# Two attention heads in two halves of the array: unpadded queries, values by query block, o rounded one slot later

## The reference, cut to what matters

```python
def index_scores(qi, wi, ki, qpos, kpos):
    s = einsum('bthd,bsd->bths', qi, ki) * (IDX_DIM ** -0.5)
    s = einsum('bths,bth->bts', relu(s), wi)
    return where(kpos <= qpos, s, MASK_VALUE)
def forget_attend(q, k, v, Fq, Fk, qpos, kpos):
    logits = einsum('bthd,bshd->bhts', q, k) * (HEAD_DIM ** -0.5)
    logits = logits + (Fq[..., None] - Fk[..., None, :])
    logits = where(kpos <= qpos, logits, MASK_VALUE)
    return einsum('bhts,bshd->bthd', softmax(logits), v)
```

## Time and profile before

| | us |
|---|---|
| three runs: median (lowest, highest) | 1118.53 (1115.49, 1121.29) |
| the profiled execution, its own time | 1120.04 |
| its span in the trace | 1118.2 |
| PE busy | 1007.4 (90%) |
| DVE busy | 577.5 (52%) |
| ACT busy | 409.9 (37%) |
| POOL busy | 183.4 (16%) |

### The profile page before, as it was taken

How to read it: one execution, slowest core, us unless ns; L and a number is a source line. 1 busy time by engine, 2 the same in 40 slices (tenths; PEclk the granted TensorE clock), 3 DMA queues, 4 the chain that set the end, 5 groups by cost and what they waited for, 6 DMA issues and landing times.

```text
span 1118.2 us, 19588 instructions
## 1 busy us (share of the span) xinstructions
PE 1007.4 (90%) x7336; PEld 911.4 (82%) x7336; DVE 577.5 (52%) x1295; ACT 409.9 (37%) x818; POOL 183.4 (16%) x127
## 2 busy tenths in 40 slices
PE   5889988898989888649989999599989999998998
PEld 4687777787778778637489999589989999998998
DVE  2634899767575662563048844664433234442232
ACT  3355454444555442112065444344421124431111
POOL 4303223322342223320002322000000000000000
PEclk9799999999999999779979999799999999998999
DMA  9521521312222225774626665223323233332322
GB/s 323 165 79 32 163 76 48 87 45 62 56 67 57 59 57 160 246 233 135 207 85 198 193 201 173 76 57 95 94 76 94 83 87 93 94 94 75 88 64 77
DMA packets 186184, 124.51 MB, mean 111 GB/s; under 512 B 16499, under 2 KB 170163, under 8 KB 186116
## 3 DMA queue, kind: packets, MB, share of 16 engines
q1 hardware_dynamic: 185986, 123.50, 36.8%
q10 hardware_dynamic: 130, 0.10, 0.0%
HBM read 116.99 MB, written 6.59 MB: 111 GB/s over the span
## 4 chain that ended last, share of the span: by engine, by line
PE 74%; DVE 9%; DMA 5%; issue 4%; SPq 3%; ACT 3%; POOL 2%; ACTq 0%; DVEq 0%; POOLq 0%
PE bank L842 19%; PE bank L843 19%; PE bank L844 19%; PE bank L922 3%; PE bank L904 3%; DMA qbc<-q_d 3%; PE bank L1069 2%; PE bank L913 2%; POOL prod L772 1%; SPq L557 1%; DVE w_lo L1658 1%; PE bank L888 1%; PE bank L885 1%; PE bank L884 1%; PE bank L887 1%
## 5 line engine op out<-in xcount | busy, mean ns | idle before, releaser
L842 PE MATMUL bank<-h_hi,w_hi 128*128 128x260 f32 x1360 | 410.5, 302 | 29.0 <-issue 14.2
L843 PE MATMUL bank<-h_lo,w_hi 128*128 128x260 f32 x1360 | 394.8, 290 | 0.0
L844 PE MATMUL bank<-h_hi,w_lo 128*128 128x260 f32 x1360 | 393.9, 290 | 0.0
L842 PEld LDWEIGHTS bank<-h_hi,w_hi 128*128 128x128 f32 x1360 | 267.6, 197 | 37.9 <-issue 30.7
L843 PEld LDWEIGHTS bank<-h_lo,w_hi 128*128 128x128 f32 x1360 | 267.7, 197 | 4.1 <-issue 2.9
L844 PEld LDWEIGHTS bank<-h_hi,w_lo 128*128 128x128 f32 x1360 | 267.2, 196 | 0.0
L742 POOL TENSOR_TENSOR w_lo<-raw,w_hi 128x1024 fp32r<-128x1024 f32 x44 | 104.9, 2383 | 396.1 <-ACT w_hi L1259 229.6
L842 PE MATMUL bank<-u_hi,w_hi 128*128 128x260 f32 x512 | 147.0, 287 | 7.7 <-DVE u_lo L2046 7.7
L2031 DVE TENSOR_TENSOR w_lo<-raw,w_hi 128x1024 fp32r<-128x1024 f32 x62 | 76.0, 1226 | 146.2 <-ACT w_hi L1490 146.2
L843 PE MATMUL bank<-u_lo,w_hi 128*128 128x260 f32 x512 | 146.3, 286 | 0.0
L844 PE MATMUL bank<-u_hi,w_lo 128*128 128x260 f32 x512 | 146.3, 286 | 0.0
(11 more groups left out here) (319 smaller groups left out, 1384.0 us busy)
## 6 DMA issues: line engine op xcount, KB each, us to landing
raw<-in_w_in SPq DMA_DIRECT2D x44, 512.0 KB, 3.7
raw<-in_w_ada SPq DMA_DIRECT2D x32, 512.0 KB, 4.1
raw<-in_w_up SPq DMA_DIRECT2D x32, 512.0 KB, 3.8
raw<-in_w_down SPq DMA_DIRECT2D x32, 512.0 KB, 3.6
ada<-in_w_ada SPq DMA_DIRECT2D x4, 2048.0 KB, 13.6
kv<-in_cache_k_b SPq DMA_DIRECT2D x16, 256.0 KB, 3.1
qbc<-q_d SPq DMA_DIRECT2D x16, 256.0 KB, 4.1
kv<-in_cache_k_a SPq DMA_DIRECT2D x16, 256.0 KB, 3.4
```

Source lines behind the costliest of these rows:

```text
L842: mm(out, hi[:, k, :], x_h, start=first and k == ks[0], stop=False)
L843: mm(out, hi[:, k, :], x_l, start=False, stop=False)
L844: end = mm(out, lo[:, k, :], x_h, start=False, stop=last and k == ks[-1])
```

## The change

Both heads of a pair are worked side by side. q_pad becomes q_fm (head 0 in rows 0 to 63, head 1 in rows 64 to 127, no padding), and scores takes both heads of one query block, each from its 64 rows, into banks 4 and 5; it runs in even slots only and waits for the logits of both units before. A unit's number now counts the head fastest: U % 2 is the head, U % 8 // 2 the block. index_scores does the same for two index heads. values is called in odd slots, four times a pair, for one query block of both heads, five units behind: each head in its half of the columns, in products of 128 columns. p_t holds two blocks in turn instead of a whole head. round_o goes to slot 3 and rest_o to slot 4. The memsets of POOL, the waits on them, and the second copies on ACT go. The place of all tiles in memory stays the same.

```diff
@@ POOL
-            pool.memset(q_idx[:, :, :], 0.0).then_inc(zeroed, 1)
...
-            pool.wait_ge(h_lo_ready, N_H)
-            pool.memset(q_pad[:, :, :, :], 0.0).then_inc(zeroed, 1)
@@ PE
+            def unit(U):
+                return U // 8, U % 2, U % 8 // 2
+
             def scores(U):
-                p, hh, qb = U // 8, U // 4 % 2, U % 4
+                p, _, qb = unit(U)
                 if U >= 2:
-                    pe.wait_ge(lg_ready, U - 1)
+                    pe.wait_ge(lg_ready, U)
                 if U % 8 == 0:
                     pe.wait_ge(back_read, 2 * p + 2)
-                mm(bank[4 + U % 2][:, 0:width(qb)], q_pad[:, p % 2, hh, qb * P:(qb + 1) * P],
-                   k_fm[:, p % 2, 0:width(qb)], start=True, stop=True).then_inc(s_done, 1)
+                for hh in range(2):
+                    rows = slice(64 * hh, 64 * hh + 64)
+                    mm(bank[4 + hh][:, 0:width(qb)], q_fm[rows, p % 2, qb * P:(qb + 1) * P],
+                       k_fm[rows, p % 2, 0:width(qb)], start=True, stop=True).then_inc(s_done, 1)
...
-            def values(p, hh):
-                pe.wait_ge(pt_ready, 8 * p + 4 * hh + 4)
-                pe.wait_ge(v_ready, p + 1)
-                if p >= 1:
-                    pe.wait_ge(o_lo_ready, p)
-                for kb in range(QB):
-                    last = mm(bank[7][64 * hh:64 * hh + 64, kb * P:SEQ], v_tok[:, p % 2, kb, 64 * hh:64 * hh + 64],
-                              p_t[:, hh, kb, kb * P:SEQ], start=kb == 0, stop=kb == QB - 1)
+            def values(U):
+
+                p, _, qb = unit(U)
+                pe.wait_ge(pt_ready, U + 2)
+                if qb == 0:
+                    pe.wait_ge(v_ready, p + 1)
+                    if p >= 1:
+                        pe.wait_ge(o_lo_ready, p)
+                for kb in range(qb + 1):
+                    for hh in range(2):
+                        rows = slice(64 * hh, 64 * hh + 64)
+                        last = mm(bank[7][rows, qb * P:(qb + 1) * P], v_tok[:, p % 2, kb, rows],
+                                  p_t[:, qb % 2, hh, kb, :], start=kb == 0, stop=kb == qb)
                 last.then_inc(pv_done, 1)
...
             def index_scores(n):
                 qb, h = 1 + n // H, n % H
                 if n >= 2:
-                    pe.wait_ge(idx_relu, n - 1)
-                mm(bank[4 + n % 2][:, 0:width(qb)], q_idx[:, h, qb * P:(qb + 1) * P], ki2[:, 0:width(qb)],
-                   start=True, stop=True).then_inc(idx_done, 1)
+                    pe.wait_ge(idx_relu, n)
+                for hh in range(2):
+                    rows = slice(64 * hh, 64 * hh + 64)
+                    mm(bank[4 + hh][:, 0:width(qb)], q_idx[rows, h // 2, qb * P:(qb + 1) * P], ki2[rows, 0:width(qb)],
+                       start=True, stop=True).then_inc(idx_done, 1)
...
-                    for n in range(3 * s, 3 * s + 3):
+                    for n in range(3 * s + s % 2, 3 * s + 3, 2):
                         index_scores(n)
...
-                if 0 <= U < N_UNITS:
+                if 0 <= U < N_UNITS and U % 2 == 0:
...
-                if s == 6 and 1 <= p <= N_PAIRS:
-                    values(p - 1, 0)
-                if s == 2 and p >= 2:
-                    values(p - 2, 1)
+                if 0 <= U - 5 < N_UNITS and U % 2:
+                    values(U - 5)
@@ ACT
             def store_pt(U):
-                p, hh, qb = U // 8, U // 4 % 2, U % 4
+                hh, qb = U % 2, U % 8 // 2
                 act.wait_ge(pt_done, U + 1)
-                if p >= 1:
-                    act.wait_ge(pv_done, 2 * (p - 1) + hh + 1)
-                A(p_t[:, hh, 0:qb + 1, qb * P:(qb + 1) * P], bank[6][:, 0:width(qb)].rearrange("p (k c) -> p k c", k=qb + 1),
+                if U >= 4:
+                    act.wait_ge(pv_done, U // 2 - 1)
+                A(p_t[:, qb % 2, hh, 0:qb + 1, :], bank[6][:, 0:width(qb)].rearrange("p (k c) -> p k c", k=qb + 1),
                   ACT.Copy).then_inc(pt_ready, 1)
...
-                    A(q_pad[0:64, p % 2, 0, :], bank[3][0:64, :], ACT.Copy, scale=gq[0:64, m:m + 1])
-                    A(q_pad[64:128, p % 2, 1, :], bank[3][64:128, :], ACT.Copy, scale=gq[64:128, m:m + 1]).then_inc(back_read, 1)
+                    A(q_fm[:, p % 2, :], bank[3][:, :], ACT.Copy, scale=gq[:, m:m + 1]).then_inc(back_read, 1)
...
-                    A(q_idx[0:64, 2 * c, lo:hi], bank[half + 4 * par(i)][0:64, 0:hi - lo], ACT.Copy)
-                    last = A(q_idx[64:128, 2 * c + 1, lo:hi], bank[half + 4 * par(i)][64:128, 0:hi - lo], ACT.Copy)
+                    last = A(q_idx[:, c, lo:hi], bank[half + 4 * par(i)][:, 0:hi - lo], ACT.Copy)
...
-                if s == 2 and p >= 2:
+                if s == 3 and p >= 2:
                     round_o(p - 2)
@@ DVE (logits and probs take the new numbering of units)
-                if s == 3 and p >= 2:
+                if s == 4 and p >= 2:
                     rest_o(p - 2)
```

26 lines of the change are left out of this document (12 added, 14 removed).

## The result

| | before | after |
|---|---|---|
| runs: median (lowest, highest), us | 1118.53 (1115.49, 1121.29) | 1125.38 (1123.07, 1126.79) |
| ratio, 95% interval | | 1.0053 (1.0031, 1.0074) |
| span of the profiled execution | 1118.2 | 1123.7 |
| mean granted clock of PE | 0.948 | 0.944 |

What follows compares the result with a forecast made beforehand. PE, with chain waits and clock falls, was taken to bound stages 3 to 8, DVE stages 1 and 2. Work and waits -10.3 us, new clock falls +7.9, front -0.4: -2.8, so 1116 us; range 1106 to 1128.

Steps and rivals of the forecast that it cites:

- Stage 0 costed at nothing: Stage 0: index scores lose about half of 15 us of PE, but stage 1's first DVE step waits for fbc anyway.
- under the same cover: Stage 0: DVE's fdiag waits for the fbc load, hiding pair waits of 1 to 1.5 us; cover gone, worth 3 to 4.
- PE's work: Stages 3 to 8, a pair: scores -2.14, values -2.13, visits to narrow tile forms +1.6, so -2.7 us; -16 in all.
- waits: Stages 3 to 8: 14.4 us in slot 5, 11.5 in slot 7, 2.5 for tok_ready and sample step, replacing 17.9.
- clock: Stages 3 to 8: half of 11 new gaps lose the clock at 1.6 us each, +7.9; old falls of 4.8 go.
- rival (3): Attention scores: half-height products don't overlap, +12.8 us on the forecast, 1128.5 us; chance 0.08.
- rival (2): Stages 3 to 8: the clock falls in nearly all 11 new gaps, +7 us, 1125.5 us; chance 0.15.
- the argument from length: PE gaps: no fall after 1.68 us, most after 3.3, so half of those of 2.0 to 2.7 us fall.
- the rule about transposes: Turns ending the gaps: a Trainium skill rule says transposes don't count as clock activity; cited for the slower rival, no size.
- Nothing moves: Ahead of PE's start at 62.59: dropping padded copies on ACT gains nothing, since DVE's w_lo sets the release.
- the root: Prediction wrong at its root if stages 5 to 8 shorten by over 2.5 us each or slot 7 has no gap.
- within: Whole kernel: a time within about 0.5% (5.6 us) of no change; chance 0.44.

Runs made afterwards that it cites:

- a_idx_four: Changed kernel with its pairs of index products on four banks instead of two, waiting for the relus of the pair before the last; 1118.39 us, ratio 0.9985.
- a_filler: Changed kernel plus two unread 128x512 products ahead of the turn in slots 5 and 7 of stages 1 to 8; 1113.96 us, ratio 0.9953.
- a_filler_behind: Changed kernel plus two unread 128x512 products behind the turn in slots 5 and 7 of stages 1 to 8; 1136.95 us, ratio 1.0169.
- a_proj57: Changed kernel with the fifth and sixth half projection of a stage in slots 5 and 7 instead of 4 and 6; 1126.95 us, ratio 1.0068.
- a_proj57_back7: Changed kernel with the last two half projections in slots 5 and 7 and the turn to features moved from slot 6 to 7; 1128.47 us, ratio 1.0068.
- a_pad_filler: Changed kernel with the old padded, single index scores and two unread products ahead of the turn in slots 5 and 7; 1107.54 us, ratio 0.9901.

## Why the prediction was wrong, step by step

In the profiled execution the forecast was -2.8 us and +5.5 came. Of these 8.3 us 5.9 lie in stage 0 and 4.2 in stages 3 to 8; stages 1 and 2 take -0.9, the stretch behind -0.9.

**Stage 0 costed at nothing: the step that failed.** Miss: 5.9 us (5.5 late against 0.4 early). The prediction saw each piece: that a pair waits for both relus of the last pair, and that fbc covers some microseconds. It priced the wait at 1 to 1.5 us "under the same cover" without adding it up over eight slots and without asking what stands on ACT between the two relus of a pair. The sum is 9.5 us of waits, and two falls of the clock on top, against a cover that ended at 124.2. Half of the 15 us of index products was to go, and with free banks most of it does (PE is busy for 30.4 us in a_idx_four). In the changed kernel PE was busy 35.8 us instead of 37.2, since about 10 us of the stage ran at 1.2 GHz, and idle 9.5 instead of 1.8. The cover itself was right (3.5 us in a_idx_four).

**Stages 3 to 8: three terms, each off by 3 to 4 us.**

| | forecast | measured | how |
|---|---|---|---|
| PE's work | -16 | -12.8 | length less waits less clock |
| waits | +10.5 | +7.5 | 27.1 - 19.6 |
| clock | +3.1 | +7.1 | (114 - 41) x 0.097 |
| sum | -2.4 | +1.8 | 230.5 - 228.7 |

PE's work: the halves do overlap and rival (3) falls. A pair of 256 wide scores, and values of 16 instructions (four products in each column half), kernel after:

```profile
393.94 0.70 PE L909 MATMUL bank<-k_fm,q_fm 64*128 64x256 f32 x4
394.58 0.60 PE L1002 MATMUL bank<-ident,z_s 128*8 128x128 f32 x4
...
398.09 1.09 PE L932 MATMUL bank<-p_t,v_tok 128*64 128x128 f32 x16
399.11 0.60 PE L1002 MATMUL bank<-ident,z_s 128*8 128x128 f32 x4
```

0.64 us for 256 columns x 1.68 = 0.43 and a visit of 0.21; 1.02 for 4 x 128 columns = 0.86 and 0.16. A second part of the price stands in front of the visit: the same turn of one block holds PE for 0.11 us ahead of full-height scores and for 0.20 ahead of half-height ones (kernel before, then after):

```profile
283.27 0.27 PE L913 MATMUL bank<-ident,lg 128*128 128x128 f32 x1
283.38 0.81 PE L904 MATMUL bank<-k_fm,q_pad 128*128 128x384 f32 x2
```

```profile
393.74 0.27 PE L918 MATMUL bank<-ident,lg 128*128 128x128 f32 x1
```

So a visit costs 0.25 to 0.30 us in all, about as dear as I took it (0.26). The Trainium skill (TensorEngine Tiling (Array Packing), Key Properties) explains such a price by a drain. Stage 5 without a fall on either side confirms the total: in a_filler it is 33.79 us long, 4.15 of them from the starts of the fillers to the turns behind them, so 29.6 us of work against 31.7 before (33.57 less the wait of 1.68 and 0.17 of the product that ends just ahead of it), 2.1 a pair as in the table (12.8 / 6); the forecast was 2.7. The missing 0.6 us a pair isn't found in these rows and stays open.

Waits: the sizes hold well in slots 5 and 7. Slot 5: 2.32, 2.31 and four of 2.05, 12.8 us (forecast 14.4); slot 7: none in stage 3, then 2.66, 1.86, 1.87, 2.40, 2.40, 11.2 us (11.5). Of the 2.5 us for tok_ready 0.47 came. One wait was put at nothing: at the end of stage 9, where round_o and rest_o now come a slot later, PE waits 1.47 us for o_hi (432.06), which the kernel before does not. The kernel before had a wait of 1.70 at 201.9, just outside the stretch of the earlier trace rows, which shrank to 1.11. The collision of DVE with POOL went where it costs nothing: the 256 wide multiplication of slot 4 takes 0.35 us as forecast, the bias behind it 2.54 us beside POOL's w_lo instead of 0.35 (stage 6, 329.58), and DVE still waits 0.22 us for PE after it.

The clock: behind the 11 new waits it fell 7 times; the forecast said half and reckoned with five (0.45 of 11). That is between my forecast and rival (2), in which I put 0.15 and for which I had said that the kernel is slower from 7 falls on. The seven cost 102 x 0.097 = 9.9 us in the projections (forecast 7.9), and the three old ones only 27 x 0.097 = 2.6 (forecast 4.8, which by the earlier trace rows included turns and scores). A fourth old fall, the one behind the side step of stage 3, has no wait in front; the prediction, which knew falls behind gaps alone, did not list it. The step that failed here is the argument from length. I ordered the waits by their length (none at 1.68, most at 3.3) and put those of 2 to 2.7 between. a_filler_behind shows that length alone isn't the variable: with 1.7 us of work behind them, 3 of the same 11 waits lose the clock, and others than before. The change took work away beside the waits (the 2.3 us of values in slot 6, between slots 5 and 7, became 0.4 in slot 5 and 0.6 in slot 7) and made two waits a stage out of one; which of the two brings the falls is not separated. The reason I gave in (2), little work between gap and gap, agrees with a_filler_behind; the rule about transposes that I put beside it does not hold here. Which of the eleven waits loses the clock (not those at 223, 309, 381 and 415) no run predicts.

**Small steps.** "Nothing moves" ahead of PE's start: 61.77 against 62.59, but the 13 other profiled kernels with the new order start between 61.86 and 62.92, the two others with the old one at 62.72 and 62.85; the difference is small and the spread as large. fdiag was forecast at 123.8 and came at 127.67. Stages 1 and 2 at 0 (within 1 us): -0.9. DVE's wait for PE below 2 us up to 197: one of 1.0. Stages 5 to 8 didn't shorten by over 2.5 us each, and slot 7 has its gap: the root held.

The ratio of 1.0053 lies at the border of "within" (0.44) and "slower" (0.22); its interval (1.0031, 1.0074) excludes "faster", to which I had given 0.34.

## What to carry to other kernels

When two products are issued together into two banks, look at who empties the banks, in what grouping, and what stands between the two on that engine: a pair waits for the later of two. Sum small waits that come every slot before calling them covered, and compare the sum with the end of the cover. If a dense engine waits once or twice a stage, its clock is a term of its own. Count its falls by the granted clock, not by one kind of instruction: the falls of a_filler_behind and a_proj57 hardly show in the projections. Put into the wait first what is due anyway (values ahead of the turn: 7.4 us in stages 3 to 8), then work that nobody needs (9.0 us there).

## What the runs showed of the hardware

- One unread product of 0.86 us in each wait of about 2 us ended all seven falls behind the waits (6 long-pitch products instead of 114, all of another fall). Work of 1.7 us behind the unchanged waits left three of the seven, at other waits.
- The clock also falls where PE does not wait: behind 3.7 us of 32 products of 8 columns it was at 0.50 (kernel before, 234.7 to 238.0), and in 15 of the 17 profiled kernels it fell during this side step or within 1.2 us of its end; in a_proj57_back7 it was low already, in a_pad_filler it did not fall.
- One fall costs about 1.6 us (1.56 by stage 5 with and without one).
- Float32 turns through PE held the clock like products (no fall behind the 11 waits with turns in them).
- Two 64-row products in the two row halves run fully side by side (0.64 us for two of 256 columns); the visit to the form costs 0.16 to 0.21 us, and the turn ahead of it 0.09 more (0.20 against 0.11).
- An operation of DVE that takes 0.35 us (128x384) took 2.54 us while POOL subtracted w_lo (kernel after, 329.58).
